# Down weights on GpSimd's DMA queue, up-weight slots handed out by halves, and the two fixed experts' tokens gathered first

## The reference

```python
def moe_swiglu(u, router_w, w1, w3, w2):        # layer 1, 8 experts, width 2816
    logits = tokens @ router_w
    top_vals, top_idx = lax.top_k(logits, TOP_K)       # TOP_K = 2
    gates = jax.nn.softmax(top_vals, axis=-1)
    ...
        return (jax.nn.silu(xb @ w1[e]) * (xb @ w3[e])) @ w2[e]

def grouped_moe(x, router_w, router_b, w_gate, w_up, w_down):   # layers A and B, 16 experts, width 512
    ...                                        # one group of 4 experts per token, then 2 of its experts
    for e in range(N_EXPERTS_2):
        h = jax.nn.silu(xt @ w_gate[e]) * (xt @ w_up[e])
        out = out + combine[:, e:e + 1] * (h @ w_down[e])
```

## Time and profile before

| what | value |
|---|---|
| time, median of 3 runs | 2474.13 us (2471.5 to 2476.7) |
| the profiled execution: its time, its span | 2472.53 us, 2470.8 us |
| TensorE matmul busy | 2208.6 us (89%) |
| TensorE weight loads, VectorE, ScalarE busy | 981.6, 498.6, 381.6 us |
| GpSimd busy | 34.6 us, 108 instructions |
| queue q1 (DMAs issued by SP) | 629.55 MB |
| queue q0 (DMAs issued by GpSimd) | 12.69 MB |
| TensorE idle ahead of L1227 for a DMA | 84.6 us |

### The profile page before, as it was taken

The page is one execution under the profiler, slowest core; times in us unless marked ns, Lnnn a source line. Parts: engine busy times, 40 slices in busy tenths (PEclk is TensorE's granted clock), DMA queues, the critical chain, the costliest instruction groups (busy, mean ns, idle before and its releaser), DMA issues. The chain is left out here.

```text
span 2470.8 us, 30992 instructions
## 1 busy us (share of the span) xinstructions
PE 2208.6 (89%) x13218; PEld 981.6 (40%) x13218; DVE 498.6 (20%) x1252; ACT 381.6 (15%) x885; POOL 34.6 (1%) x108
## 2 busy tenths in 40 slices
PE   4999998999999899999999999987787878867787
PEld 1574543444875333222222222245432327432232
DVE  2143850001195200000000000012311122130113
ACT  2013431001242311000000000022111010110101
POOL 2000000000000000000000000000000000000000
PEclk9999999999999899999999999997898889878899
DMA  8131358434655589999999999850699972079993
GB/s 301 68 110 63 134 206 288 153 119 142 216 213 179 205 316 359 356 368 378 358 369 369 356 387 356 320 209 0 277 381 412 404 303 105 34 305 382 408 403 119
DMA packets 249755, 644.32 MB, mean 261 GB/s; under 512 B 10995, under 2 KB 50379, under 8 KB 233227
## 3 DMA queue, kind: packets, MB, share of 16 engines
q1 hardware_dynamic: 245675, 629.55, 68.0%
q0 software_dynamic: 3936, 12.69, 1.5%
HBM read 641.15 MB, written 1.05 MB: 260 GB/s over the span
## 5 line engine op out<-in xcount | busy, mean ns | idle before, releaser
L1227 PE MATMUL bank<-ring,wide 128*32 128x512 f32 x5888 | 670.4, 608 | 86.7 <-DMA ring<-in_w_up 84.6
L1227 PEld LDWEIGHTS bank<-ring,wide 128*32 128x32 f32 x5888 | 189.3, 112 | 539.2 <-issue 526.6
L1254 PE MATMUL bank<-dreg,RB 128*32 128x512 f32 x2944 | 339.1, 596 | 0.0
L2735 DVE TENSOR_TENSOR H<-SG,bank 128x256 f32<-128x256 f32 x92 | 38.8, 421 | 1041.1 <-ACT SG L1879 1041.1
L1879 ACT ACTIVATE SG<-bank 128x256 f32<-128x256 f32 x92 | 35.3, 383 | 1017.3 <-PE bank L1227 1017.3
L845 PE MATMUL bank<-wide,ring 128*128 128x256 f32 x832 | 182.2, 381 | 0.6 <-ACT wide L1648 0.6
L845 PEld LDWEIGHTS bank<-wide,ring 128*128 128x128 f32 x832 | 158.6, 191 | 24.1 <-issue 2.2
L835 PE MATMUL bank<-ring,wide 128*128 128x512 f32 x352 | 156.8, 604 | 1.2 <-DMA ring<-in_w_kv 1.0
L1254 PEld LDWEIGHTS bank<-dreg,RB 128*32 128x32 f32 x2944 | 84.2, 109 | 185.2 <-issue 184.8
L1144 PE MATMUL bank<-ring,wide 128*128 128x512 f32 x352 | 154.6, 592 | 0.9 <-ACT wide L1648 0.9
L835 PE MATMUL bank<-ring,T 128*128 128x512 f32 x256 | 115.8, 613 | 1.6 <-ACT sm L2084 0.8
(11 more groups left out here) (434 smaller groups left out, 1453.2 us busy)
## 6 DMA issues: line engine op xcount, KB each, us to landing
ring<-in_l_moe_w SPq DMA_DIRECT2D x160, 1024.0 KB, 8.5
dreg<-in_l_moe_w SPq DMA_DIRECT2D x88, 1024.0 KB, 13.7
ring<-in_w_gate SPq DMA_DIRECT2D x64, 1024.0 KB, 10.2
ring<-in_w_up SPq DMA_DIRECT2D x64, 1024.0 KB, 12.3
dreg<-in_w_down SPq DMA_DIRECT2D x64, 1024.0 KB, 9.5
ring<-in_l_mod_w SPq DMA_DIRECT2D x24, 2048.0 KB, 8.1
ring<-in_l_ffn_w SPq DMA_DIRECT2D x22, 1024.0 KB, 10.1
ring<-in_l_moe_w SPq DMA_DIRECT2D x32, 512.0 KB, 7.6
```

The source lines that it names most:

```text
L1227: mm = pe.matmul(banks[r % 2][32 * g:32 * g + 32, :].rearrange("p (w n) -> p w n", w=2), tokens_of(m.order[i][0], c, k), w, start=k == 0, ...
L1254: mm = pe.matmul(banks[4 + 2 * (m.unit(m.order[i][0]) % 2) + h][32 * g:32 * g + 32, :], HQ[:, r % 4, j, 32 * q:32 * q + 32], dring[:, i % ...
L2735: i = dve.tensor_tensor(H[:, r % 2, :], SG[:, r % 2, :], banks[r % 2][:, FSTEP:NCH], ALU.mult)
```

## The change

It has three parts.

1. The down loads of all three mixtures leave SP and are issued by GpSimd (`down_loads`), in GpSimd's own program order, with the same wait for the block 4 earlier. SP's loads are now gate and up weights alone. `down_follows` is gone.
2. The gate and up slots are handed out by halves, in the order `halves`: sorted by the round in which the pair begins, then by half, then by pair. Where two pairs begin in one round (2 and 3, 6 and 7, 10 and 11, 14 and 15 of MOEA and MOEB) the order becomes low, low, high, high in place of low, high, low, high; the rest stays, and in MOE1 no two pairs begin in one round.
3. In MOEA and MOEB the tokens of places 0 and 1 are gathered first, alone (`GATHERS2`): their one-hots are made before `order_experts` runs, and 16 matmuls stand ahead of round 0. Those of places 2 to 4 are another 16 matmuls, between rounds 0 and 1.

```diff
@@ class Moe @@
+        begins = [self.pair_rounds(q)[0] for q in range(self.pairs)]
+        self.halves = sorted(((q, h) for q in range(self.pairs) for h in range(2)), key=lambda a: (begins[a[0]], a[1], a[0]))
...
+    def slot(self, q, h):
+        return self.halves.index((q, h)) % RING
...
-QUARTERS2 = [range(0, 5), range(5, 10), range(10, 15), range(15, 16)]
+GATHERS2 = [range(0, 2), range(2, 5), range(5, 10), range(10, 15), range(15, 16)]
+GATHER_HOME = [(0, 0), (0, 4 * 32), (1, 0), (0, 0), (1, 0)]
+GATHER_PARTS = [(0, 0, 4), (0, 4, 4), (1, 0, 4), (1, 4, 4)] + [(g, k, 2) for g in (2, 3) for k in range(0, KC, 2)] + [(4, 0, 4), (4, 4, 4)]
...
+        def down_loads(eng, m, w2, numbers):
+
+            known = {}
+            for i in numbers:
+                s, (p, st) = i % RING, m.order[i]
+                e, f = expert_at(eng, m, known, p), slice(st * FSTEP, (st + 1) * FSTEP)
+                if i >= RING:
+                    eng.wait_ge(sem("moe_down_done"), m.before["down_done"] + i - RING + 1)
+                eng.dma_start(dring[:, s, :, :], w2(e)[f, :].rearrange("(j p) n -> p j n", p=P)).then_inc(sem(f"moe_down_in{s}"), 16)
@@ SP @@
+            def expert_loads(m, w1, w3):
+
+                known = {}
+                for n, (q, h) in enumerate(m.halves):
+                    slot = n % RING
+                    if n < RING:
+                        slot_free(slot)
+                    else:
+                        last_q, last_h = m.halves[n - RING]
+                        passed = ("upped_low", "upped")[last_h]
+                        sp.wait_ge(sem(f"moe_{passed}"), m.before[passed] + max(m.pair_rounds(last_q)) + 1)
...
@@ GpSimd @@
             gate_rows(GATED[4:])
+            pool.wait_ge(sem("x_updated"), 3)
+            down_loads(pool, MOE1, lambda e: A["l1_moe_w2"][e], range(RING))
 
             wait_output(pool, GAP5[-1] + "T")
...
             step(i, "order_made")
+            down_loads(pool, MOE1, lambda e: A["l1_moe_w2"][e], range(RING, MOE1.blocks))
...
             rows_after(5, [(0, 0, A["ln2_b_2"][0], D), (1, 0, A["ln1_g_2"][1], D), (2, 0, A["ln1_b_2"][1], D)])
+            down_loads(pool, MOEA, lambda e: A["w_down_2"][0, e], range(MOEA.blocks))
...
+            pool.wait_ge(sem("x_updated"), 7)
+            down_loads(pool, MOEB, lambda e: A["w_down_2"][1, e], range(MOEB.blocks))
@@ PE, paired_rounds @@
-                    for n in range(4):
-                        gather_quarter(n, banks[4 + n])
+                    for n in range(2):
+                        gather_part(n, banks[4 + n])
...
+                        if r == 0:
+                            for n in (2, 3):
+                                gather_part(n, banks[4 + n])
@@ DVE @@
                 if m is not MOE1:
+                    step(dve.tensor_copy(at_place[:, :, 0:m.fixed], place[:, :, 0:m.fixed]))
+                    one_hots(m, 0)
                     return
...
-                one_hots(m, 0)
                 one_hots(m, 1)
+                one_hots(m, 2)
```

More of the change, by code:

```diff
@@ L77, in counts @@
         n |= {name: 4 * self.units for name in ("scattered", "added")}
-        n |= {"all_placed": 4 * TT if sorted_here else TT, "down_done": self.blocks}
-        n |= {f"up_in{p}": self.loaded(self.pairs - 1 - (self.pairs - 1 - p) % 2) for p in range(2)}
+        n |= {"all_placed": len(GATHERS2) * TT if sorted_here else TT, "down_done": self.blocks}
+        n |= {f"up_in{s}": self.loaded(*self.halves[len(self.halves) - RING + s]) for s in range(RING)}
         n |= {f"down_in{s}": 16 * len(range(s, self.blocks, RING)) for s in range(RING)}
@@ L87, in runs, with loaded @@
         return [(a, lo, 2 * FSTEP, 0)] if a == b else [(a, lo, FSTEP, 0), (b, lo2, FSTEP, FSTEP)]
-    def loaded(self, q):
-        return sum(2 * 16 * len(self.runs(p)) for p in range(q % 2, q + 1, 2))
+    def slot(self, q, h):
+        return self.halves.index((q, h)) % RING
+    def loaded(self, q, h):
+        n = self.halves.index((q, h))
+        return sum(2 * 16 * len(self.runs(p)) for p, _ in self.halves[n % RING:n + 1:RING])
     def in_pair(self, i):
@@ L484, in spilled, with gather_width, gathered_at, expert_at @@
             return eng.value_load(flag[0:1, MOES.index(m):MOES.index(m) + 1], min_val=0, max_val=1)
[L486 to L492, removed]
+        def gather_width(m, g):
+            return 32 * sum(m.sizes[p] for p in GATHERS2[g])
+        def gathered_at(m, p):
+            g = [g for g in range(len(GATHERS2)) if p in GATHERS2[g]][0]
+            home, at = GATHER_HOME[g]
+            return g, home, at + 32 * (m.first_chunk[p] - m.first_chunk[GATHERS2[g][0]])
+        def expert_at(eng, m, known, p):
+            if p < m.fixed:
+                return p
+            if p not in known:
+                i = MOES.index(m)
+                eng.wait_ge(sem("ordered"), i)
+                known[p] = eng.value_load(held[0:1, i - 1, p:p + 1], min_val=0, max_val=m.experts - 1)
+            return known[p]
+        def down_loads(eng, m, w2, numbers):
[6 more added lines that the diff above has]
+                eng.dma_start(dring[:, s, :, :], w2(e)[f, :].rearrange("(j p) n -> p j n", p=P)).then_inc(sem(f"moe_down_in{s}"), 16)
         def unrolled(m):
@@ L590, in dense_loads @@
                     holder[st % RING] = ("upped", TT * (st + 1))
[L592 to L651, removed]
@@ new lines, in expert_loads @@
+            def expert_loads(m, w1, w3):
[8 more added lines that the diff above has]
+                        sp.wait_ge(sem(f"moe_{passed}"), m.before[passed] + max(m.pair_rounds(last_q)) + 1)
+                    for i, w in enumerate((w1, w3)):
+                        for p, lo, width, at in m.runs(q):
+                            rows = w(expert_at(sp, m, known, p)).rearrange("(k p) n -> p k n" if m is MOE1 else "(p k) n -> p k n", p=P)
+                            sp.dma_start(pairs[:, slot, i, :, at:at + width], rows[:, 4 * h:4 * h + 4, lo:lo + width]).then_inc(
+                                sem(f"moe_up_in{slot}"), 16)
```

77 lines of the change are left out of this document (38 added, 39 removed).

## The result

The changed kernel takes 2456.64 us (median of 4 runs, 2453.96 to 2464.78) against 2474.06 for the kernel before (4 runs beside it): ratio 0.9936, 95% interval 0.9915 to 0.9956. A second set (`after_again`) gave 0.9946 (0.9932 to 0.9959). The profiled execution is the slowest of its four: 2464.8 us, span 2463.1, against 2470.8 before. So its trace shows 7.7 us of gain where the median has some 16.

The account below looks back on a forecast made before the run. MOE1 bound by TensorE, MOEA and MOEB by their weights' transfers. MOEA -2.3 + 1.4, MOEB -3.8 + 1.4, MOE1 +1.5 sum to -1.8 us: 2470.7 us profiled, median 2472, range 2461 to 2484.

Parts of the forecast that it names:

- the DMA share is 1.01 and 1.00: MOEA and MOEB middles, at 409 and 407 GB/s: only an earlier continuous stream or earlier last gate and up weights win time.
- theory 1: Follow-up forecast, MOEA and MOEB: SP waits on down loads while slots are free; own queue lifts stream to about 417 GB/s.
- The gaps, forecast at -2.3 and -3.8: Dry stream before and behind round 2: MOEA 8.5 us to one gap of 6.2, MOEB 18.8 us to 15.0.
- round 2's low half frees two slots, before the stream dries: MOEA: round 2's low half runs at 1800 to 1803.4, the stream would dry at 1806, so the gap behind goes.
- Clock behind a wait inside a round, +1.4 each: End of MOEA and MOEB: last high half takes 5.8 us behind its wait if the clock falls, +1.4 us a layer.
- The down queue's share, term 0: MOEA and MOEB: down queue gets a third of the stream, 26 down loads in at the end as before, 0 us.
- The half share: Rival, MOEA and MOEB: down queue takes half the stream, 4.1 us later in each layer, 2480 us; 10 in 100.
- the last rival's overtaking: Last gate and up loads overtake down loads, 24 or 25 in at the end, 2462 to 2467 us; 16 in 100.
- No down matmul waits: MOEA and MOEB: two down loads take 15 us at a third of the stream, over 25 us are there before use.
- Another of these signs: Sign of being wrong: the time from round 2 to round 11 changes by more than 3 us.
- MOE1, +1.5: MOE1: down loads share the stream with the second pair's gate and up loads; 0 to +4 us, taken as +1.5.
- The narrow gather by width: Rival: a narrow gather costs by its width, round 1 begins 5 us earlier than before, 2456 us; 8 in 100.

Follow-up runs that it names:

- after_again: The changed kernel run once more with no edit, against the kernel before: 2457.14 us, ratio 0.9946.
- own_queue_only: The kernel before with only part 1, all down loads on GpSimd's queue: 2467.45 us, ratio 0.9979.
- Q1, Q2 and H: Own down queue in MOE1, own down queue in MOEA and MOEB, and slots by halves; together against the kernel before: 2455.56 us, ratio 0.9927.
- halves_only: The kernel before with only the gate and up slots by halves, down loads still on SP's queue: 2473.94 us, ratio 1.0008.
- halves_and_fixed: The changed kernel without the own queue, all down loads on SP as before: 2471.69 us, ratio 0.9997 to the kernel before.
- first_queue_only: The kernel before with MOE1's down loads alone on GpSimd's queue, MOEA and MOEB untouched: 2475.75 us, ratio 1.0010.
- later_queue_halves: The kernel before with the own queue in MOEA and MOEB alone and slots by halves, no added gather: 2451.08 us, ratio 0.9916.

## Why the prediction was wrong

**The bound was read rightly.** MOEA and MOEB go by their weights; every variant that gained there gained by dry time or by rate.

**The step that failed first: "the DMA share is 1.01 and 1.00", so only the stream's start and the order at its end could win time.** The sum had no term for the rate of the full stream. Before, the middle of the layers held short dips that a mean over 180 us doesn't show: of 78 windows of 2 us in the 156 us, 7 in MOEA and 5 in MOEB lie below 390 GB/s, the lowest at 246 and 203, while the middle one has 417. In `own_queue_only` none does (lowest 397 and 393), and the middle one has 416. So the queues together are not faster than one at its best; the dips are gone. One of them, before: SP had issued its last load at 1849.42 and then waited for round 5's low half, up to 1869.37 (packets by queue, MB, share, from 1869.5 to 1871.5):

```profile
DMA packets 117, 0.53 MB, mean 266 GB/s; under 512 B 14, under 2 KB 14, under 8 KB 92
## 3 DMA queue, kind: packets, MB, share of 16 engines
q1 hardware_dynamic: 116, 0.52, 93.1%
```

The same place in `own_queue_only`, where the gate and up loads were issued at 1867.62 (1866 to 1870):

```profile
DMA packets 422, 1.63 MB, mean 409 GB/s; under 512 B 36, under 2 KB 36, under 8 KB 409
## 3 DMA queue, kind: packets, MB, share of 16 engines
q0 software_dynamic: 400, 1.53, 95.4%
q1 hardware_dynamic: 22, 0.11, 6.5%
```

The share of 93% misleads: it counts the time that the packets took, and those of 8 KB took 552 ns on average from 1870 to 1872, against 317 over the 156 us. The bytes show the dip. In `own_queue_only` the gate and up queue is just as empty, but the down queue's backlog fills the engines. Another dip, from 1956 to 1962 (317, 348 and 340 GB/s in its three windows), came as theory 1 has it. Pair 14 takes the slots of pair 12, which round 9 was done with at 1950.1; but SP stood at the wait of a down load, and pair 14's loads went out 10.3 us later. SP's queue before, and the same loads in `own_queue_only`, where round 9 ended at 1951.4:

```profile
1944.76 0.38 SPq L617 DMA_DIRECT2D ring<-in_w_up  x1
1956.33 3.29 SPq L626 DMA_DIRECT2D dreg<-in_w_down  x2
1960.44 0.34 SPq L617 DMA_DIRECT2D ring<-in_w_gate  x1
...
1948.72 0.33 SPq L629 DMA_DIRECT2D ring<-in_w_gate  x1
1949.15 0.38 SPq L629 DMA_DIRECT2D ring<-in_w_up  x1
1951.58 0.33 SPq L629 DMA_DIRECT2D ring<-in_w_gate  x1
```

A third cause may share in it. In that dip, from 1958 to 1962, nearly all packets were those of down loads, near 4 KB:

```profile
DMA packets 352, 1.38 MB, mean 344 GB/s; under 512 B 18, under 2 KB 18, under 8 KB 350
q1 hardware_dynamic: 352, 1.38, 95.3%
```

Of the 156 windows of both layers before, 33 have over 0.9 of their bytes in such packets at a share of 0.97 or more; they average 404 GB/s, where the 77 with almost only 8 KB packets average 421. In `own_queue_only`, where the two sorts are mixed, 2 windows are of the first kind. By that, some 2 us of the loss in both layers would be the price of small packets alone and not of an empty queue; no run separates the two. The term is some 180 us of full stream x (1 - 409/417) = 3.5 us in MOEA, and with 407 4.3 us in MOEB.

The Trainium skill (DMA: Bandwidth & Descriptors, section Issuing engines are not separate DMA queues) says that issuing DMAs on several engines at once saves only the time that the issuing takes. Here, where a stretch went from 409 and 408 to 417 GB/s with the same loads, the second queue was worth more: a backlog that stays while the other queue waits.

**The gaps, forecast at -2.3 and -3.8, measured at -4.4 and -5.4** (8.9 to 4.5 and 18.9 to 13.5 by the table's measure, profile of after). The size was off by some 2 us in each layer, and so was the cause, in the main. The prediction gave the gain to the early round 0. Part 3 alone brings 0.3 and 1.5, beside Q1, Q2 and H nothing beyond the spread (4.3 and 14.1 without it, 4.5 to 4.9 and 13.2 to 13.5 with it), since its second gather adds to TensorE's work ahead of round 2. Beside the own queue without the halves it does bring something: 0.2 and 3.6 us of dry time, and 5.7 us by the ratios (0.9979 to 0.9956). So parts 2 and 3 win in part the same time. What closes the stretch behind round 2 is the order low, low, high, high *with* the own queue: without part 3, dry times go from 8.8 and 18.6 to 4.3 and 14.1. The order without the own queue leaves 2.8 us of that stretch in MOEA (`halves_only`, 1811 to 1817). The prediction had the mechanism of that stretch ("round 2's low half frees two slots, before the stream dries") and put it down as a part of the same gain.

**Clock behind a wait inside a round, +1.4 each: as forecast.** The last high half took 5.93 us behind its wait (3.64 undisturbed, 5.8 assumed), and its low half had run before the wait. The gather took 7.88 us (8.5 assumed), that between the rounds 9.94 (8.0 and a later row's 2.2).

With the two terms put right, MOEA is -4.4 - 3.5 + 1.4 = -6.5 (measured -6.2), MOEB -5.4 - 4.3 + 1.4 = -8.3 (-8.4). That close an agreement is luck in part: three profiles with the same code in MOEA gave 279.4, 278.9 and 275.7 us. With MOE1's +2.5 (below) the sum is -12.3, where the two ratios of the whole change give -15.8 and -13.4.

**The down queue's share, term 0: right for the share, a little off for the order.** In 1820:1986.5 the down queue moved 23.13 of 69.31 MB, exactly a third, in 5988 packets beside 6348: nearly one for one. The half share did not take place. At the last gate and up landing 26 down loads were in, as forecast, in MOEA of this profile and in both layers of all five profiles without the own queue; but 25 in its MOEB and in 16 of the 18 layers of the nine profiles with the own queue, the 26th landing 0.2 to 2.1 us later. So a small part of the last rival's overtaking did happen, worth less than the 2.6 us of one load in a layer.

**"No down matmul waits": wrong.** A down load of 1 MiB took a median of 14.8 and up to 29 us to land, and the text allowed 15. It was one of the prediction's own signs of being wrong. What the 35.3 us of waits cost isn't shown; the gate and up waits gave up 58 meanwhile. Another of these signs came true too: from the end of round 2 to that of round 11 MOEA took 184.2 us before and 179.9 after, 4.3 less where 3 were allowed.

**MOE1, +1.5: right in sign.** `first_queue_only` has +2.5 (0 to 4.9). From MOE1's first round to MOEA's first transpose (851.94 to 1748.22, 896.3 us, before) the six profiles with its down loads on GpSimd have 896.6 to 899.6 us, mean 898.2, the eight without 894.5 to 896.4, mean 895.7: 2.5 us.

**The narrow gather by width: no.** 32 rows took 7.88 us at 128 wide, 0.246 us each; the earlier trace rows had 0.25 at 96. This rival's 2456 is the number that came nearest the measured 2456.6 and 2457.1, by luck: what it rests on did not happen.

**Left open.** Queue and halves without part 3 gain more than dry time and rate give: for `later_queue_halves` 4.1 + 4.9 + 3.5 + 4.3 - 2.8 = 14.0, against 20.8 (17.6 to 24.0) by the ratio and 8.4 + 10.0 = 18.4 in its two layers (277.2 and 276.6 us). The added gather may cost what is missing in the changed kernel, and the 25 down loads in place of 26 may give some of it; no run separates these. And `own_queue_only` had MOEB at 285.0 us, 1.6 shorter, and MOEA at 280.3, 5.3 shorter, where the rate gives 4.3 and 3.5: the sum fits and the parts don't, which may be the spread of single profiles.

## What to carry to other kernels

Where a stage goes by its transfers, look at the full stream in windows of 2 us, not at one mean share: dips of a few us, two of them traced here to one in-order queue behind a wait with nothing more issued, were worth some 8 us here by the rates and 5.4 by the medians of `own_queue_only`, and a second queue with a backlog removed them. A slot comes free when the work ahead of it is done. So moving the gather about ahead of round 2 gained nothing here; less of it shortened the dry time, and so did freeing both low halves first, beside the own queue. And parts of a change don't add up: halves were worth 0 alone and 0.5% beside the own queue, so test them in pairs, and leave out those that bring nothing (without MOE1's queue and the added gather it is 2451 us).

## What was unexpected of the hardware

With 4 KB packets on one queue and 8 KB ones on the other, the two together moved 417 GB/s in every variant and stretch, with no window below 390; one queue alone had 417 as its middle value, with dips down to 203 (111 in `halves_and_fixed`). And two profiles of one and the same kernel differed by 8.8 us of span, of which 1.6 lay in the two layers, so stages are to be compared, not spans; and a stage with unchanged code still differed by up to 3.7 us.
